# Expert sums in a PEER layer: every fourth pair of slots of the first two tiles summed on VectorE instead of TensorE

## The reference, cut to what matters

```
def _peer(h, p):
    ...
    best, pos = lax.top_k(cand, PK_TOPK)
    eidx = jnp.take_along_axis(cidx, pos, axis=-1)
    gate = jax.nn.softmax(best, axis=-1)
    ...
    def block(args):
        hb, eb, gb = args
        act = jax.nn.gelu(jnp.einsum('td,thkd->thk', hb, u_tab[eb]).astype(jnp.float32))
        return jnp.einsum('thk,thkd->td', (gb * act).astype(hb.dtype), v_tab[eb])
```

## Time and profile before

| | |
|---|---|
| Median of 3 runs | 4029.2 us (4024.41 to 4033.59) |
| The profiled execution | 4030.63 us, its span 4028.8 us |
| TensorE busy, mean granted clock | 2988.6 us (74%), 0.865 |
| VectorE busy | 2791.5 us (69%) |
| Share of the chain that ended last | DMA 39%, TensorE 35%, VectorE 12% |
| Moved by all DMA | 1346.46 MB, of it 1208.03 MB by the gathers |
| First gather of the expert sums | shortly before 1000 us |

### The profile page before, as it was taken

The page is one execution under the profiler, slowest core; times in us unless marked ns, Lnnn a source line. Parts: engine busy times, 40 slices in busy tenths (PEclk is TensorE's granted clock), DMA queues, the critical chain, the costliest instruction groups (busy, mean ns, idle before and its releaser), DMA issues.

```text
span 4028.8 us, 44643 instructions
## 1 busy us (share of the span) xinstructions
PE 2988.6 (74%) x15418; PEld 1226.2 (30%) x15418; DVE 2791.5 (69%) x6862; ACT 686.7 (17%) x1416; POOL 1324.7 (33%) x1174
## 2 busy tenths in 40 slices
PE   8988989997889998885666666656666666665555
PEld 3655656454434443221221111111111111111111
DVE  4635446657577777764888877877886877787555
ACT  2433434011112121000120110110111101011000
POOL 0000000003334443442444444444444444444443
PEclk9999999998989998997888877878887888787777
DMA  4010000649899999999999999999999999999998
GB/s 180 22 37 21 22 16 34 250 168 368 336 402 413 416 416 401 419 420 421 408 400 419 413 414 418 412 410 414 414 414 413 417 411 406 416 419 406 418 419 345
DMA packets 214320, 1346.46 MB, mean 334 GB/s; under 512 B 24738, under 2 KB 45730, under 8 KB 63170
## 3 DMA queue, kind: packets, MB, share of 16 engines
q0 software_dynamic: 165888, 1208.03, 72.9%
q1 hardware_dynamic: 48196, 135.41, 9.0%
HBM read 1329.69 MB, written 13.67 MB: 333 GB/s over the span
## 4 chain that ended last, share of the span: by engine, by line
DMA 39%; PE 35%; DVE 12%; issue 10%; POOL 2%; ACT 1%; POOLq 0%; SPq 0%; DVEq 0%; ACTq 0%
DMA arena<-in_uv,mask_b 14%; PE ps L771 12%; DMA arena<-in_uv,mask_f 12%; DMA arena<-in_uv,ones 10%; PE ps L1434 10%; DVE arena L1289 3%; PE ps L749 3%; PE ps L632 3%; POOL arena L610 2%; DMA arena<-in_w_q 2%; DVE arena L1167 2%; PE ps L1428 2%; PE ps L691 1%; PE ps L659 1%; PE ps L1481 1%
## 5 line engine op out<-in xcount | busy, mean ns | idle before, releaser
L771 PE MATMUL ps<-arena 64*64 64x512 f32 x9216 | 1456.9, 759 | 919.4 <-DVE arena L1167 907.4
L1289 DVE CUSTOM_DVE_ANT_0 arena<-arena 128x1024 f32<-128x1024 f32 x1152 | 1411.9, 1226 | 742.4 <-DMA arena<-in_uv,mask_b 289.8
L771 PEld LDWEIGHTS ps<-arena 64*64 64x64 f32 x9216 | 351.3, 158 | 1896.9 <-DVE arena L1167 1372.6
L610 POOL DMA_INDIRECT arena<-in_uv,ones x384 | 443.2, 1154 | 658.4 <-PE ps L771 501.4
L610 POOL DMA_INDIRECT arena<-in_uv,mask_f x384 | 443.6, 1155 | 582.0 <-PE ps L771 490.4
L610 POOL DMA_INDIRECT arena<-in_uv,mask_b x384 | 432.2, 1125 | 588.2 <-PE ps L771 499.8
L964 ACT ACTIVATE arena<-arena 128x2 f32<-128x2 f32 x576 | 117.2, 203 | 2601.1 <-DVE arena L1289 2600.9
L1434 PE MATMUL ps<-arena 128*128 128x384 f32 x1152 | 392.7, 498 | 16.4 <-issue 14.7
L1167 DVE TENSOR_SCALAR arena<-arena 128x64 f32<-128x64 f32 x1152 | 308.0, 310 | 14.9 <-ACT arena L964 14.9
L594 POOL IOTA arena<- 128x16 f32 x1 | 0.1, 144 | 846.6 <-PE ps L641 846.6
L749 PE MATMUL ps<-arena 128*128 128x384 f32 x768 | 270.0, 498 | 2.2 <-ACT arena L893 2.2
(11 more groups left out here) (206 smaller groups left out, 2485.5 us busy)
## 6 DMA issues: line engine op xcount, KB each, us to landing
arena<-in_w_mod SPq DMA_DIRECT2D x12, 2048.0 KB, 23.2
arena<-in_w_mg SPq DMA_DIRECT2D x16, 1536.0 KB, 20.2
arena<-in_w_in SPq DMA_DIRECT2D x28, 512.0 KB, 3.3
arena<-in_w_out SPq DMA_DIRECT2D x2, 4096.0 KB, 17.9
arena<-in_w_q SPq DMA_DIRECT2D x8, 1024.0 KB, 19.4
arena<-in_w_q SPq DMA_DIRECT2D x4, 2048.0 KB, 34.4
arena<-x_scratch SPq DMA_DIRECT2D x15, 512.0 KB, 11.2
arena<-in_uv,ones POOLq DMA_INDIRECT x384, 10.4
```

The source lines that it names most:

```text
L610: nc.gpsimd.indirect_dma_start(out=RG[n % RING], out_offset=None, in_=uv, in_offset=bass.IndirectOffsetOnAxis(ap=EIDX[t % 3][:, s:s + 1], ...
L771: mm = nc.tensor.matmul(PS[c * HALF:(c + 1) * HALF, 2 * r + n, :], DG[rows, s, :], RG[s][rows, D + n * 512:D + (n + 1) * 512], start=(g == ...
L1289: ins = v.tensor_tensor_reduce(u, u, h2, 1.0, 0.0, ALU.mult, ALU.add, PRE[:, s % RING:s % RING + 1])
```

## The change

In tiles 0 and 1, from group 37 on, each group whose number in its tile has remainder 2 by 4 is taken off TensorE: groups 38, 42, ... 62 of tile 0 (7 groups) and 66, 70, ... 126 (16 groups), 23 groups and 46 slots. For such a group `coef` makes no diagonals. It multiplies gelu and gate of its two slots (128x2), waits for that, and adds the two `v` halves, scaled by a number for each partition, onto an accumulator `ACC` of 128x1024 in SBUF: the first slot of a tile with a `tensor_scalar`, each other one with a `scalar_tensor_tensor` that reads and writes ACC. The last raises `v_summed`, for which POOL waits, in place of `v_used`, before it refills those two buffers. `products` is left out for such a group, and every wait on `v_used` and `diag_ready` counts TensorE's slots alone. `add_sums` of tiles 0 and 1 gets one more addition, of ACC, behind a wait for its own first one.

```diff
+SUM_FROM, SUM_EVERY = 37, 4
...
+def on_dve(n):
+
+    t, g = divmod(n, GROUPS)
+    return t < EARLY - 1 and n >= SUM_FROM and g % SUM_EVERY == 2
...
+    ACC = MG[:, :, 2 * P:3 * P]
...
-                    wait_alone(pool, v_used, n + 1 - RING)
+                    if on_dve((n - RING) // GRP):
+                        wait_alone(pool, v_sum, dve_groups((n - RING) // GRP + 1))
+                    else:
+                        wait_alone(pool, v_used, pe_slots(n + 1 - RING))
...
             n0 = t * SLOTS + g * GRP
+            if on_dve(t * GROUPS + g):
+                return
...
-            pe.wait_ge(diag_r, n0 + GRP)
+            pe.wait_ge(diag_r, pe_slots(n0 + GRP))
...
+        def sum_group(n):
+
+            t, g = divmod(n, GROUPS)
+            m, s0 = dve_groups(n), n * GRP % RING
+            v.tensor_tensor(COEF, GEL[:, s0:s0 + GRP], GATE[t % 3][:, g * GRP:(g + 1) * GRP],
+                            ALU.mult).then_inc(coef_r, 1)
+            dve.wait_ge(coef_r, m * GRP + 1)
+            for k in range(GRP):
+                rows = in_strips(RG[s0 + k][:, D:2 * D])
+                if k == 0 and not dve_groups(t * GROUPS) < m:
+                    if m == 0:
+                        dve.wait_ge(q_r, len(QUERY_ORDER))
+                    ins = v.tensor_scalar(ACC, rows, COEF[:, 0:1], None, ALU.mult)
+                else:
+                    if k == 0:
+                        dve.wait_ge(v_sum, m)
+                    ins = v.scalar_tensor_tensor(out=ACC, in0=rows, scalar=COEF[:, k:k + 1], in1=ACC,
+                                                 op0=ALU.mult, op1=ALU.add)
+                if k == 0:
+                    ins.then_inc(coef_r, 1)
+                    dve.wait_ge(coef_r, m * GRP + 2)
+            ins.then_inc(v_sum, 1)
...
             dve.wait_ge(gel_r, n + 1)
+            if on_dve(n):
+                sum_group(n)
+                return
...
                 ins = v.tensor_tensor(self.y, self.y, self.z, ALU.add)
+                if self.t < EARLY - 1:
+                    dve.wait_ge(v_sum, dve_groups((self.t + 1) * GROUPS))
+                    ins.then_inc(sum_z, 1)
+                    dve.wait_ge(sum_z, self.t + 1)
+                    ins = v.tensor_tensor(self.y, self.y, ACC, ALU.add)
```

13 lines of the change are left out of this document (10 added, 3 removed).

## The result

| | before | after |
|---|---|---|
| Median of 7 runs each, same chip | 4030.37 us (4024.41 to 4033.59) | 4043.05 us (4037.37 to 4047.43) |
| Ratio after to before, 95% interval | | **1.0028** [1.0019, 1.0038] |
| Span of the profiled execution | 4028.8 us | 4042.7 us |
| TensorE busy | 2988.6 us | 2953.9 us |
| VectorE busy | 2791.5 us | 2840.1 us |

The changed kernel is slower by 0.28%, 12.7 us. So some 11 us are to be explained, where +2.5 was summed up.

What follows compares the result with a forecast made beforehand. The prediction took the gathers' DMA rate as the bound, with TensorE late in a few windows. Its terms, +2.2 + 2.3 - 2.0 = +2.5 us on the profiled 4030.6, gave 4033.1, set to 4032 us against the median; range 4022 to 4045.

Steps and rivals of the forecast that it cites:

- the bound of 0.2%: Whole kernel: about 8 us is the least difference a measurement can tell; slower than 4037 us had 0.26.
- Rival 2: Eight groups with a long step: VectorE's bursts empty the ring, DMA idles 18.6 us less 2.0, 4046 us; chance 0.15.
- What bounds it: Group 38 to end of tile 1: gathers at 418 GB/s set the pace; five short windows lose 8.0 us.
- The price on VectorE: In the 23 groups and at two tile ends: 55.2 us more VectorE time, 2.33 us for most groups.
- The gain at 1180 to 1220, -2.0 us: Windows at 1180 and 1200 us: VectorE can just follow, so half of TensorE's 3.9 us is gained, 2.0.
- The gain in the dense stretch given up, and 2.2 us lost: From 1503 to 1585 us: 9.3 us of sums against 7.1 of waits, 2.2 us longer; TensorE's 2.8 not had.
- Eight long groups, +2.3 us: Eight groups where a sum meets a long VectorE step: 2.3 us added for all, the worth of one sum.
- The addition at the tile end, hidden: Ends of tiles 0 and 1: 2.6 us of accumulator additions, counted as hidden in VectorE's waits for gathers.
- Rival 1, the relief comes through: Short DMA windows: VectorE's lag stays inside the ring and TensorE's relief brings 8.0 us, 4021 us; chance 0.12.
- Rival 3, the clock: TensorE among the merges: its clock falls in pauses, three groups at the lower level cost 16 us, 4045; chance 0.06.
- Rival 4, the issues: POOL's gather issues: 44 sums lengthen them by 0.98 us each without cover, 43 us, 4072 us; chance 0.03.
- the ring: Gather buffers in tiles 0 and 1: 8 slots, taken as a cover of 20.1 us against late refills.

Runs made afterwards that it cites:

- e11: The change with sums only in tile 0, at seven other groups, and the accumulator added in VectorE's copy out of PSUM: 4030.79 us, 1.0002 to the kernel before.
- e1: The change with its 23 groups neither multiplied on TensorE nor summed on VectorE, tile-end additions kept: 4032.28 us, 0.9995 to the kernel before.
- e12: The change with its 23 sums moved to groups where VectorE has most other work: 4038.17 us, 1.0018 to the kernel before.
- e10: The change with its 23 groups at other places and the accumulator added in VectorE's copy out of PSUM: 4028.67 us, 0.9998 to the kernel before.
- e6: The change with TensorE multiplying zeros into the same banks in place of the missing products: 4040.42 us, 1.0036 to the kernel before.
- e4: The change with each sum replaced by a reduction of the same rows with one SBUF input: 4037.19 us, 1.0014 to the kernel before.

## Why the prediction was right in part and wrong in part

The time came out at 4043.05, inside the range of 4022 to 4045, at its upper end, and 11 us above the forecast. That it lies inside is owed to the room left for the rivals and not to the sum, which came to 2.5 us where 10 to 13 were measured. By the bound of 0.2% the likeliest outcome, with 0.68, was no difference; 0.28% lies beyond it, in "slower", for which I had 0.26. Rival 2 (4046) is nearest, by time and by its sign, but not by the mechanism that it gave.

- **What bounds it: right.** The gathers pace tiles 0 and 1, and a shortfall of DMA windows is the measure of loss. Over the stretch 37 to 153 no kernel is more than 1.6% above before.
- **The price on VectorE: right.** 1.285 us for a sum (1.28), 0.155 for the small product, 0.754 for the first one (0.81), 8.60 us for group 99 (8.7). VectorE's busy time rose by 48.6 us; 55.2 had been summed up with own waits, which are not busy. The two extra additions took 1.33 us each with their waits, as summed up (1.22 + 0.1). The waits for gathers fell from 92.5 to 52.8 us, not to the 40 or so that I named.
- **The gain at 1180 to 1220, -2.0 us: right in size up to group 53, but it doesn't last.** -1.6 and -1.7 there in the two executions of the change, -3.0 at best (e11). e1 gained 2.9 and had lost 4.7 by group 97 with nothing added on VectorE, a loss that the sum has no term for.
- **The gain in the dense stretch given up, and 2.2 us lost: direction right, size wrong.** 97 to 113 cost 3.9 and 4.2 us. I had counted work against slack over the whole stretch. What the rows show on top: behind a skipped group TensorE pauses, and its next products take up to 3.69 us (+1.7) and raise POOL's semaphore the later. And the 2.8 us that I thought TensorE could give back there but for VectorE aren't there: e1, without any sum, has -0.2.
- **Eight long groups, +2.3 us: too small.** The pieces 53 to 97 and 113 to 125, where five of them lie, cost 4.9 and 2.9 us together in the two executions of the change. But e1, without any sum, has 3.9 there, and e12 puts sums beside long steps with no more loss than the change. So that the long groups make this loss isn't shown; the term was laid on the wrong thing.
- **The addition at the tile end, hidden: wrong.** This is the step that failed clearly. I set 2.6 us of additions against 92.5 us of waits between 1190 and 1640; the second addition is at 1703, where the timeline has no wait at all. It lengthened groups 129 to 132 by 1.3 us in every kernel that has it, and dropping both additions brought 6 us (2 to 10) by the ratios.
- **The sum by its terms**: -1.7 for -2.0, +4.0 for +2.2, +3.9 (the mean of 4.9 and 2.9) for +2.3, +3.2 for 0, and -1.0 behind group 137: 8.4 us, the mean of 9.6 and 7.2, where I had 2.5. The 3.2 us are those of the piece 125 to 137; 1.3 of them are the addition.
- **Rival 1, the relief comes through**: it didn't, in the change or in e10, the best kernel (0.9998 [0.9988, 1.0008]). What the relief alone is worth stays open: e1 is at 0.9995 where 0.998 was the price, but it still had the extra additions, and that kernel wasn't run without them.
- **Rival 3, the clock**: its mechanism is in the trace, and I had dismissed it on the ground that the pauses would be 1.9 us at most. Ahead of the eight slow products they are 2.0 to 6.3 us: the merges of two groups follow each other, and the next diagonals don't come earlier. But the count of slow products over all kernels doesn't go with the loss, and e6 brought no time back, so it is unlikely to be the greater part; e6 is no pure test.
- **Rival 4, the issues**: not seen. The mean issue is 1.14 us before and after, and its price of 43 us never came near; 1.0014 for e4 against 1.0028 doesn't separate the two. The rule of the Trainium skill in "SBUF — State Buffer", section "Who interferes with whom", by which a VectorE instruction with two SBUF inputs contends with a GpSimd instruction that reads SBUF, but not with one that only writes it, is neither borne out nor refuted by that: no row shows what an issue reads.
- **Slower by rival 2's mechanism**: a lag that leaves the ring empty, seen at 1520 to 1530 (336 and 317 GB/s). Its account by long groups doesn't hold (e12). That its price of 16.6 us came near the 10 to 13 measured is luck in part, since the tile ends, which it has at nothing, paid a share.

## What to carry to other kernels

Slack must be counted where the added instruction stands, and to the last one: an addition of 1.2 us, in a stretch without a wait, made the four groups around it longer by its full length in each of ten kernels, and by the ratios the two additions cost about as much as the placement of forty-six sums. Taking work off an engine that waits for another's per-group result bought a pause in front of that result here, not an earlier one; look first whether the result itself is late (group 99 was, with and without the sums). Where a resource outside both engines sets the pace, there is little for moving work between them to win: the kernel with other places and no extra pass came out even (0.9998), and that is no reason to change. And look at what an edit does on the other engine: half a group of products took TensorE as long as a whole one (1.93 and 1.95 us).
